# A hybrid GLA, sparse-attention and sliding-window step on one core: norm rows waited for later, a second raw weight buffer, index dots moved to GpSimd, page loops in groups of four

## The reference, cut to what matters

```python
def indexer_scores(iq, iw, ik):
    dots = relu(einsum('bqhd,bsd->bqhs', iq, ik))        # 8 index heads of 64
    return einsum('bqhs,bqh->bqs', dots, iw)             # weighted sum over heads

def dsa_prompt(q, k, v, iq, ik, iw):                     # per block of 128 queries
    sc = where(key_pos <= t, indexer_scores(iqb, iwb, ik), -inf)
    _, idx = top_k(sc, 256)
    return dsa_attend(qb, k[idx], v[idx], idx <= t)

def dsa_sample(...):                                     # keys and values through a page table
    ik_past = cache_idx[layer, page_table].reshape(Bd, 2048, 64)
    ...                                                  # the same search over past and new keys
    ks = where(in_past, cache_k[layer, phys, off], k_new[...])
    vs = where(in_past, cache_v[layer, phys, off], v_new[...])

def trunk(x, ...):                                       # for each of the two layers
    h = layer_norm(ALPHA * x + mix, ln_g[l, 0], ln_b[l, 0])
    x = layer_norm(ALPHA * h + swiglu(h, w_gu[l], w_down[l]), ln_g[l, 1], ln_b[l, 1])
```

## Time and profile before

| What | us |
|---|---|
| median of three runs | 3891.2 |
| the profiled execution | 3894.8 |
| its span, first to last instruction | 3893.2 |
| TensorE busy | 3341.4 (86%) |
| VectorE busy | 1649.4 (42%) |
| ScalarE busy | 1045.0 (27%) |
| GpSimd busy | 311.5 (8%) |
| mean granted TensorE clock | 0.893 of full speed |

### The profile page before, as it was taken

How to read it: one execution, slowest core, us unless ns; L and a number is a source line. 1 busy time by engine, 2 the same in 40 slices (tenths; PEclk the granted TensorE clock), 3 DMA queues, 4 the chain that set the end, 5 groups by cost and what they waited for, 6 DMA issues and landing times. The chain is left out here.

```text
span 3893.2 us, 53928 instructions
## 1 busy us (share of the span) xinstructions
PE 3341.4 (86%) x20627; PEld 2846.7 (73%) x20627; DVE 1649.4 (42%) x2937; ACT 1045.0 (27%) x2064; POOL 311.5 (8%) x421
## 2 busy tenths in 40 slices
PE   7896885646778888899999998894999899999997
PEld 7686764433344444799999998792566899999997
DVE  2175662217688775211112565341454311112566
ACT  2212542102132232211111444311443211112443
POOL 2200111310000000000000001260000000000002
PEclk8997885876788777899999999895999899999999
DMA  4111004340000000111112110213000111112111
GB/s 125 44 34 40 23 12 119 105 137 22 26 18 8 19 17 6 54 43 43 43 48 79 51 58 33 55 34 127 16 27 28 56 47 43 43 43 92 39 58 47
DMA packets 232352, 190.71 MB, mean 49 GB/s; under 512 B 49538, under 2 KB 210580, under 8 KB 232148
## 3 DMA queue, kind: packets, MB, share of 16 engines
q1 hardware_dynamic: 216436, 166.17, 14.1%
q0 software_dynamic: 8832, 19.02, 1.6%
q10 hardware_dynamic: 6912, 3.15, 0.3%
HBM read 158.64 MB, written 31.38 MB: 49 GB/s over the span
## 5 line engine op out<-in xcount | busy, mean ns | idle before, releaser
L1849 PE MATMUL ffn1u_ps<-h_hi,ffn1u_whi 128*128 128x384 f32 (+1 forms) x1056 | 348.2, 330 | 8.7 <-DVE h_lo L1911 8.7
L1849 PE MATMUL ffn0u_ps<-h_hi,ffn0u_whi 128*128 128x384 f32 (+1 forms) x1056 | 344.8, 327 | 8.9 <-DVE h_lo L1911 8.9
L1849 PE MATMUL ffn1u_ps<-h_lo,ffn1u_whi 128*128 128x384 f32 (+1 forms) x1056 | 348.1, 330 | 0.0
L1849 PE MATMUL ffn1u_ps<-h_hi,ffn1u_wlo 128*128 128x384 f32 (+1 forms) x1056 | 347.9, 329 | 0.0
L1849 PE MATMUL ffn0u_ps<-h_hi,ffn0u_wlo 128*128 128x384 f32 (+1 forms) x1056 | 344.9, 327 | 0.0
L1849 PE MATMUL ffn0u_ps<-h_lo,ffn0u_whi 128*128 128x384 f32 (+1 forms) x1056 | 344.8, 326 | 0.0
L184 PE MATMUL ine_ps<-ine_w_hi,ine_x_hi 128*128 128x256 f32 (+2 forms) x864 | 267.8, 310 | 10.5 <-ACT H L225 5.6
L184 PE MATMUL ine_ps<-ine_w_hi,ine_x_lo 128*128 128x256 f32 (+2 forms) x864 | 252.3, 292 | 0.0
L184 PE MATMUL ine_ps<-ine_w_lo,ine_x_hi 128*128 128x256 f32 (+2 forms) x864 | 251.5, 291 | 0.0
L1849 PEld LDWEIGHTS ffn1u_ps<-h_hi,ffn1u_whi 128*128 128x128 f32 x1056 | 198.9, 188 | 9.1 <-DVE ffn1u_wlo L1893 9.1
L1849 PEld LDWEIGHTS ffn0u_ps<-h_hi,ffn0u_whi 128*128 128x128 f32 x1056 | 198.7, 188 | 9.2 <-DVE ffn0u_wlo L1893 9.2
(11 more groups left out here) (438 smaller groups left out, 7354.9 us busy)
## 6 DMA issues: line engine op xcount, KB each, us to landing
ffn0u_raw<-in_ffn_w_gu_dram SPq DMA_DIRECT2D x44, 512.0 KB, 3.8
ffn1u_raw<-in_ffn_w_gu_dram SPq DMA_DIRECT2D x44, 512.0 KB, 3.8
ffn0d_w<-in_ffn_w_down_dram SPq DMA_DIRECT2D x88, 128.0 KB, 2.1
ffn1d_w<-in_ffn_w_down_dram SPq DMA_DIRECT2D x88, 128.0 KB, 2.2
ine_w<-in_w_in_even_dram SPq DMA_DIRECT2D x9, 1024.0 KB
smp_Vp<-in_cache_v_dram POOLq DMA_DIRECT2D x96, 64.0 KB, 2.2
scratch_h<-ine_stage SPq DMA_DIRECT2D x20, 256.0 KB, 2.4
smp_Kp<-in_cache_k_dram SPq DMA_DIRECT2D x80, 64.0 KB, 1.9
```

What stands on the lines that cost most here:

```text
L1849: last = nc.tensor.matmul(ps[:, t, k2, 0:n], wp[:, k2, k, :], hp[:, k, t0:t0 + n], start=(k == 0 and j == 0), stop=(k == KD - 1 and j == 2))
```

## The change

1. `load_pages` runs a quarter as many iterations; each reads four table entries and then issues four transfers.
2. The in-projection has a second raw weight buffer, in the first block only. Chunks 0 to 9 alternate (chunk 9 and later use the first one). `load_w` of chunk c up to 9 waits for the splits of chunk c-2. Three small buffers of the index part (`hit`, `oth`, `bias`) are laid over `rel`.
3. In the prompt's attention and in the sliding-window layer the norm rows have a semaphore of their own, `gain_in`, waited for where they are first used; X tiles have one semaphore per buffer.
4. In the prompt's attention a dot's multiply-add leaves VectorE. ScalarE, after the relu, multiplies by the head's weight in place; GpSimd makes the table of head weights once per block, and copies the first head's dots into `sc` or adds the others to it. New semaphores order this: `weighted`, `dot_scaled`, and `search_begun`, which keeps GpSimd from overwriting `sc` before the search has read it.

```diff
 def load_pages(eng, pages, n_pool, b, j0, j1, cache, dst_of, landed):
-    with eng.Fori(j0, j1) as j:
-        page = eng.value_load(pages[0:1, bass.ds(j + b * PAGES, 1)], min_val=0, max_val=n_pool - 1)
-        src = cache[bass.ds(page, 1)]
...
-        eng.dma_start(dst_of(bass.ds(j, 1)), src).then_inc(landed, 16)
+    group = 4
+    with eng.Fori(j0 // group, j1 // group) as g:
+        at = [eng.value_load(pages[0:1, bass.ds(g * group + (b * PAGES + r), 1)], min_val=0, max_val=n_pool - 1) for r in range(group)]
+        for r in range(group):
+            src = cache[bass.ds(at[r], 1)]
...
+            eng.dma_start(dst_of(bass.ds(g * group + r, 1)), src).then_inc(landed, 16)
...
+        def side(c):
+            return 0 if c >= CW else (CW - c) % 2
...
         def load_w(sp, c):
-            if c >= 1:
+            if c > CW:
                 sp.wait_ge(w_split, KD * c)
+            elif c >= 2:
+                sp.wait_ge(w_split, KD * (c - 1))
             for a, b, n in PROJ[c][1]:
-                sp.dma_start(raw[:, :, a:a + n], w_v[:, :, b:b + n]).then_inc(w_in, 16)
+                sp.dma_start(raw_of(c)[:, :, a:a + n], w_v[:, :, b:b + n]).then_inc(w_in[side(c)], 16)
...
+            raws.append(isb("w", [P, KD, NP]))
...
+            hit, oth = relb[:, 0, 0:TOPK], relb[:, 1, 0:TOPK]
...
+            bias = relb[:, :, :].rearrange("p a n -> p (a n)").bitcast(BF16)[:, 0:LH]
...
                 for k, w in enumerate(("ln_g", "ln_b")):
-                    sp.dma_start(gb[:, k, :], bcast_rows(A[w][0, 0], D)).then_inc(cin, 16)
+                    sp.dma_start(gb[:, k, :], bcast_rows(A[w][0, 0], D)).then_inc(gain_in, 16)
...
                         nc.scalar.activation(rel[:, d % 4, 0:n], ps[:, dot_bank[u], 0:n], ACT.Relu).then_inc(dot_read, 1)
+                        if u[2:] == (0, 0):
+                            act.wait_ge(weighted, BLOCK.index(u[1]) - 1)
+                        act.wait_ge(dot_read, d + 1)
+                        nc.scalar.activation(rel[:, d % 4, 0:n], rel[:, d % 4, 0:n], ACT.Copy,
+                                             scale=iws[:, u[2]:u[2] + 1]).then_inc(dot_scaled, 1)
...
             @block.gpsimd
             def _(pool):
-                pool.wait_ge(cin, 48)
...
                 def add_dots(u):
                     _, t, h, c = u
                     d, n = dot_no[u], min(512, (t + 1) * P - 512 * c)
                     if h == 0 and c == 0:
                         if d == 0:
-                            dve.wait_ge(ki_in, 32)
-                        link(nc.vector.tensor_scalar(iws[:, :], KI[:, t, kcol(C_IW):kcol(C_IW) + 8], IWS, None, ALU.mult))
+                            pool.wait_ge(ki_in, 32)
+                        else:
+                            pool.wait_ge(dot_scaled, d)
+                        nc.gpsimd.tensor_scalar(iws[:, :], KI[:, t, kcol(C_IW):kcol(C_IW) + 8], IWS, None,
+                                                ALU.mult).then_inc(weighted, 1)
                     part = sc[:, 512 * c:512 * c + n]
-                    dve.wait_ge(dot_read, d + 1)
+                    pool.wait_ge(dot_scaled, d + 1)
                     if h == 0:
-                        nc.vector.tensor_scalar(part, rel[:, d % 4, 0:n], iws[:, h:h + 1], None, ALU.mult).then_inc(dots_added, 1)
+                        if d > 0 and c == 0:
+                            pool.wait_ge(search_begun, BLOCK.index(t) - 2)
+                        nc.gpsimd.tensor_copy(part, rel[:, d % 4, 0:n]).then_inc(dots_added, 1)
                     else:
-                        dve.wait_ge(dots_added, d)
-                        nc.vector.scalar_tensor_tensor(out=part, in0=rel[:, d % 4, 0:n], scalar=iws[:, h:h + 1], in1=part,
-                                                       op0=ALU.mult, op1=ALU.add).then_inc(dots_added, 1)
+                        pool.wait_ge(dots_added, d)
+                        nc.gpsimd.tensor_tensor(part, rel[:, d % 4, 0:n], part, ALU.add).then_inc(dots_added, 1)
+
+                def shift(j):
+                    r = rows(out_tile[j])
+                    pool.wait_ge(scaled, j + 1)
+                    nc.gpsimd.tensor_tensor(X[0:r, j % RING_X, :], X[0:r, j % RING_X, :], gb[0:r, 1, :], ALU.add).then_inc(norm_done, 1)
+
+                for u in passes(-1):
+                    if u[0] == "dots":
+                        add_dots(u)
+                pool.wait_ge(gain_in, 32)
+                for i in range(NT):
+                    if i >= 1:
+                        shift(i - 1)
+                    for n in range(NH):
+                        for u in shares(i)[n][0]:
+                            if u[0] == "dots":
+                                add_dots(u)
+                for j in range(NT - 1, NO):
+                    shift(j)
+
+            @block.vector
+            def _(dve):
+                link = chained(dve, dch)
+                dve.wait_ge(cin, 16)
...
                     nc.vector.tensor_scalar(mv[0:r, j, 1:2], mv[0:r, j, 1:2], LN_EPS, None, ALU.add).then_inc(var_ready, 1)
+                    dve.wait_ge(gain_in, 32)
                     link(nc.vector.scalar_tensor_tensor(out=x, in0=x, scalar=mv[0:r, j, 0:1], in1=gb[0:r, 0, :],
                                                         op0=ALU.subtract, op1=ALU.mult))
...
                     link(nc.vector.match_replace(wk[:, 0:L], m8[:, :], src[:, 0:L], TAKEN))
+                    if k == 0:
+                        dve.sem_inc(search_begun, 1)
...
             def _(dve):
                 link = chained(dve, dch)
                 copy = nc.vector.tensor_copy
-                dve.wait_ge(cin, 64)
+                dve.wait_ge(cin, 32)
```

More of the change, by code:

```diff
@@ L108, in even_in @@
     width = [max(a + n for a, _, n in pieces) for _, pieces in PROJ]
-    landed = [16 * sum(len(PROJ[d][1]) for d in range(c + 1)) for c in range(NCH)]
+    landed = [16 * sum(len(PROJ[d][1]) for d in range(c + 1) if d > CW or (CW - d) % 2 == (CW - min(c, CW)) % 2)
+              for c in range(NCH)]
     w_v = A["w_in_even"][0].rearrange("(k p) n -> p k n", p=P)
@@ L191, in split_hi @@
             if k == 0:
-                act.wait_ge(w_in, landed[c])
+                act.wait_ge(w_in[side(c)], landed[c])
             if g >= RING:
                 wait_block(act, g - RING)
-            nc.scalar.copy(w_hi[:, g % RING, 0:width[c]], raw[:, k, 0:width[c]]).then_inc(w_split_hi, 1)
+            nc.scalar.copy(w_hi[:, g % RING, 0:width[c]], raw_of(c)[:, k, 0:width[c]]).then_inc(w_split_hi, 1)
         def split_lo(eng, subtract, c, k):
@@ L1417, in residual @@
+                for j in range(NT - 1, NO):
[4 more added lines that the diff above has]
+                dve.wait_ge(cin, 16)
+                link(nc.vector.tensor_copy(identb[:, :], st.ident[:, :]))
+                link(nc.vector.memset(bias[:, 1, 0:P], 0.0))
+                for t in range(2):
+                    nc.vector.tensor_copy(bias[:, t, t * P:(t + 1) * P], causal[:, :]).then_inc(b_done, 1)
                 def residual(u):
@@ L1463, in row_max @@
                                             ALU.mult).then_inc(m_done, 1)
-                for u in passes(-1):
-                    if u[0] == "dots":
-                        add_dots(u)
                 for i in range(NT):
```

52 lines of the change are left out of this document (22 added, 30 removed).

## The result

| | before | after |
|---|---|---|
| median, compared on one chip, us | 3891.4 | 3799.4 (3798.5 to 3801.6) |
| profiled execution / its span, us | 3894.8 / 3893.2 | 3798.5 / 3796.9 |
| TensorE, VectorE busy, us | 3341.4, 1649.4 | 3327.2, 1601.5 |
| ScalarE, GpSimd busy, us | 1045.0, 311.5 | 1095.4, 394.2 |
| mean granted TensorE clock | 0.893 | 0.907 |

The ratio is 0.976, 95% interval 0.9743 to 0.9777: 92 us less, 16 us above the forecast of 3783, inside the range. The changed kernel was timed again beside experiments (3798.2 us, ratio 0.9751, interval 0.9736 to 0.9765). The kernel before had medians of 3895 to 3897 beside the experiments, so kernels that were timed at different times are compared by stages or ratios rather than by medians alone.

The account below looks back on a forecast made before the run. Bound by TensorE in projection and feed-forwards, page waits in the sample stage, TensorE and VectorE waiting for each other in sparse attention. 8+23+10+20+14.5+33 = 108.5 us off 3894.8 gives 3786.3, less 3.6 for the median: 3783, range 3762 to 3820.

Parts of the forecast that it names:

- Index pages: In-projection: the last 32 index-key pages, issued by POOL, come 7 us sooner, plus 1 us of clock: 8 us.
- Two raw buffers: In-projection: a second raw weight buffer removes waits for evictions and low parts, and slow-clock matmuls: 10 us, bounds 5 to 12.
- Sample pages: Sample attention: shorter page loops on ScalarE, SP and POOL remove TensorE's page waits: 23 us, bounds 0 to 28.
- 0.22 us a page: Page loops: assumed saving per page, three quarters of a loop step of 0.3 us; bounds nothing to 0.65.
- Odd layer: Odd layer's start: VectorE no longer stands until the norm's bias row lands: 20 us, bounds 15 and 21.
- Opening: Start of the prompt's sparse attention: first row maximum and search come earlier, sixteen dots on ScalarE and POOL: 14.5 us, bounds 10 to 17.
- Tiles: Sparse-attention tiles: VectorE sheds 39 us of dot work, of which 33 us arrive; bounds 12 and 42.
- 85%: Sparse-attention tiles: the assumed share of VectorE's 39 us of shed work that shortens the stage, giving 33 us.
- TensorE takes over the tiles: Rival, sparse-attention tiles: only the tile ends give, 12 us instead of 33, so 3804; chance 0.21.
- The page loop gets no shorter: Rival, page loops: load latency and issue are the period, so 31 us of pages go: 3814; chance 0.12.
- The projection: Rival, in-projection: SP still sits in a store or page loop when the second buffer is free: 3793; chance 0.04.
- Slower through GpSimd: Rival, sparse attention: POOL adds stretched by VectorE's search hold ScalarE's relus and exponentials: 3906 at 7 us an add; chance 0.03.

Follow-up runs that it names:

- early copies: Changed kernel, but in the sample stage ScalarE copies the first eight groups of keys before issuing its second sixteen pages: 3796.9 us, ratio 0.9749.
- other queues: Changed kernel, with the sample stage's V pages of sequence 5 issued by ScalarE and of 6 by GpSimd, leaving SP only 7's: 3791.3 us, ratio 0.9733.

## Why the prediction was right in direction and 16 us off

The profiled span fell by 96.3 us, not 108.5; the other 4 us of the miss are the two profiled executions' distances from their medians (3.6 above, 0.9 below). Undone one at a time, the parts are worth 24.1 us (pages), 10.0 (second raw buffer), 20.1 (odd norm rows) and 20.5 (dots' move); the kernel with the dots back on VectorE is 24.1 shorter than the kernel before in this stage, by the late rows. Together this is 98.8 against 96.3, so no large part is unexplained.

- **Index pages, 8: right.** Undoing the page loops gave 8.8 in the projection. TensorE's wait fell from 9.0 to 2.3.
- **Two raw buffers, 10: right.** 10.0 by the experiment. The composition was a little different: the waits for evictions went (5.6) as forecast, that for low parts hardly moved (4.9 to 4.6, where 2.7 had been counted), and TensorE's busy time fell by 5.6, more than the 4.2 us of clock counted for both parts.
- **Sample pages, 23: the term that failed.** "I take 0.22 us a page" was too much. The step of the loop was guessed well (0.3 us, against 0.26 on SP). What failed is that all else stays: on SP and GpSimd the rest of a page became some 0.07 us longer in most groups of sixteen pages, and on ScalarE the step itself is only 0.18. A page takes SP 1.34 us, not 1.26. Over whole queues, from the table's issue: SP's 112 pages end at 159.5 us instead of 176.4 (0.15 a page), POOL's 96 at 136.5 instead of 148.9 (0.13), ScalarE's first 32 at 44.3 instead of 47.1 (0.09). So ScalarE gave 2.8, not 7.0, and POOL's V pages end 12 us earlier, not 21. From this it follows that the wait for V pages does not go: it fell from 8.0 to 4.9. Behind it TensorE goes on 138.5 us after the table's issue instead of 150.4, which is 11.9 of the stage's 13.1. The kernels with early copies and with other queues show that POOL's queue is the bound now.
- **Odd layer, 20: right.** 19.9 in the trace; 20.1 in the experiment's trace, 16 to 19 by its times.
- **Opening, 14.5: right in sum, 16.0.** The working hid two terms of opposite sign: 22.3 for the late rows and -6.3 for the dots' move. An add came every 1.41 us, not 1.33. TensorE's first scores and the row maximum waited for ScalarE's relu, not for the last add; the search waited for that and gained 13.3.
- **Tiles, 33: 28.7, of which 26.8 is the dots' move.** VectorE shed 37 us of busy time, as counted (39), and three quarters arrived instead of 85%. The place was wrong. The prediction took the 43.7 us at the tile ends as the sign that VectorE is last there, with some 4 us a tile of turnaround, and expected them to fall to that. VectorE is last there indeed, but with the search, some 35 of the 43.7 us, and no dot lies behind a tile's last row maximum, so moving the dots could not touch them; the turnaround is 0.9 us where no search runs. What fell were the waits for exponentials, 24.2 us, because ScalarE gets the row maximum sooner. That the sum came out near 33 all the same is partly luck: one factor, 85%, stood for both places. The other error is that the prediction put ScalarE's added time at nothing: without the scaling pass the tiles are 4.1 us shorter (3.3 of it in the first two) and the opening 2.6. The 4.1 are the size of what the tiles fell short, 4.3; how the pass costs them, with a lower granted clock of TensorE in the first two tiles, is not explained.
- **Rivals.** TensorE takes over the tiles: no; 28.7 is near the 33. The page loop gets no shorter: no, but it had part of it, for the saving is the loop's step alone. The projection: no. Slower through GpSimd: no; of the 42 adds of 512 columns the 24 that run beside VectorE's search take 1266 to 1277 ns, the others 1262 to 1273, and twice the adds leave all tiles from the third on as they are.

GpSimd is about twice as slow as VectorE with two inputs, says the Trainium skill (GPSIMD Engine Reference, Engine selection); here 1.27 us for GpSimd's add against 0.75 for VectorE's multiply-add is 1.7, and yet the move pays in the tiles and costs in the opening: it depends on which engine is last, not on the ratio. Issuing transfers from several engines only saves the sequencer's time, which is usually small beside the transfer itself, says the Trainium skill (DMA: Bandwidth & Descriptors, Issuing engines are not separate DMA queues); here that time is 1.3 to 1.4 us per page of 64 KB, against 1.9 to 2.3 us from issue to landing, and bounds the stage, and dealing 32 of the pages out otherwise was worth 7 us.

## What to carry to other kernels

Count a queue's issues over its whole length, per engine, and ask which queue ends last after the change: a cheaper loop shortens all of them, and the stage gains only what its last one gains. Price a move of work at each place where it stands: the same dots cost 6 us where the old engine was idle and gave 27 where it was last. A wait at a tile's end for the engine that you relieve is no promise of a gain: look at what that engine runs during the wait. Here it was the search and not the dots, which the trace before shows too. By these rows, scaling the tile ahead of its last search rounds could be worth part of these 35 us, an estimate from the waits; no run here tried it.

## What was not expected of the hardware

- The same loop edit saved SP 0.15 us a page, GpSimd 0.13 and ScalarE 0.09. The loop's step itself is 0.26, 0.25 and 0.18 us, three quarters of which would be 0.20, 0.19 and 0.14. The branch instruction in it takes 0.045 us by the trace. The Trainium skill (Advanced Engine Details and Errata, Control Flow Timing) gives about 108 ns for a compare-and-branch, more than the instruction's row and less than the whole step.
- A table load right ahead of its transfer and four loads ahead of four transfers take the same time (21.9 and 21.7 us for 16 pages).
- ScalarE takes 0.72 us for the scaling of 128x512, from SBUF to SBUF, and 0.59 for the relu of as much, from PSUM to SBUF. The scaling also reads a factor for each partition; no run tells which of the two makes it longer.
- Left open: why a page takes 0.07 us longer in some groups of sixteen; why two tiles run at a granted clock of 0.82 and 0.78 without the scaling passes and 0.73 and 0.72 with them.
